# Skipping empty slots in the indirect DMAs, and writing expert rows plainly into a two-half DRAM scratch

## The chip, the cores and the metric

One core of a Trainium2 chip runs the kernel. The metric is the device time of one execution in microseconds (us). The five engines are TensorE (PE, with its weight loads PEld), VectorE (DVE), ScalarE (ACT), GpSimd (POOL) and SyncE (SP). SP computes nothing here: it issues most DMAs. All DMAs of the core run on the same 16 DMA engines; those that SP issues are queue q1 in the profile, those that ACT issues q10, those that POOL issues q0.

## The reference, cut to what matters

One layer for 512 tokens of width 1024: a Mamba-2 mixer, a layer norm, and a mixture of 16 experts in 4 groups. Every token picks one group and 2 experts in it, so there are 1024 assignments. The second half of the computation is what the change touches:

```python
x = layer_norm(DEEPNORM_ALPHA * x + (1.0 + g1) * y, ln1_g[i], ln1_b[i])
hin = (x * (1.0 + sc2) + sh2).reshape(bsz * seq, d)
eid, wts = route(hin, router_w, router_b)          # 2 experts of one group for each token
y = moe_ffn(hin, eid, wts, w_up[i], w_down[i])      # sum over a token's two experts of w * FFN_e(hin)
x = layer_norm(DEEPNORM_ALPHA * x + (1.0 + g2) * y, ln2_g[i], ln2_b[i])
...
def expert_block(args):                             # 128 rows of one expert
    xb, e = args
    gate, up = jnp.split(xb @ w_up[e], 2, axis=-1)  # w_up[e] is 1024 x 2048
    return (jax.nn.silu(gate) * up) @ w_down[e]     # w_down[e] is 1024 x 1024
```

All is float32. Output: (1, 512, 1024) float32.

## The kernel before, in words

**Mixer, then router.** The mixer runs group by group (4 groups of 8 heads) and adds its output into `oacc` in SBUF. Then the first layer norm leaves its rows, without gain and bias, in `xt`, the modulated rows go to the DRAM tensor `h2d` (SP, L389), and the router computes `mask` (which experts a token uses), `wts` and the position of each token among its expert's rows.

**Blocks.** Experts are worked through in blocks of 128 slots, block b being expert b mod 16, `nblk` blocks in all (16 in the profiled run, one for each expert). `tab` holds four columns for each token and expert: token number, the weight in two parts, and the slot in the block. POOL's `select(n)` (L519) compares the slot column to `iota` and makes a 0/1 matrix `sel`; PE's `slot_rows(n)` (L1518) multiplies it by `tabc`, which gives for every slot the token and the weight; DVE's `slots(n)` (L1182) turns that into `idx[:, n]` and `wslot[:, n]`. An empty slot gives a zero, and `dumpc` and the offset in column 0 turn it into a row of its own at or above row 512 (`DUMP`). Both DRAM tensors have 128 such rows more than the 512 tokens need. Slots are filled from partition 0 upward.

**One block.** POOL's `gather(n)` (L508) fetches 128 rows of 4 KB from `h2d` into `xg` by an indirect DMA. PE turns them (`turn_rows`), multiplies by the up weights in 8 units of 1 MB, turns the hidden rows, and multiplies by the down weights in 4 units of 1 MB. Each product is made of three matmuls on a high and a low part: ACT copies a weight unit to its high part (`high`, L749), DVE subtracts it for the low part (`low`, L1118). Weights arrive in a ring of 4 slots of 1 MB (`ring`); SP loads the unit four places later when `low` has released a slot (L379 and L382). The split weights `wr` have 4 slots as well. The order on PE is: up of block b, with `turn_hidden(b-1)` after its unit 1 and `slot_rows(b+2)` after its unit 4, then `turn_rows(b+1)`, then down of block b-1. ACT's `evacuate(b-1)` (L781) scales the result into `yblk` at the end of its turn of block b. POOL's `scatter(b-1)` (L544) adds these 128 rows to the DRAM tensor `ysum` by an indirect DMA with `compute_op=ALU.add`; the next scatter waits for it to land. POOL's order in one turn is `gather(b+1)`, `select(b+2)`, `widen(b)`, `scatter(b-1)`. `widen` puts gain and bias of the first norm on one sixteenth of the columns, from `xt` into `x1`.

**Start values.** `ysum` has to be zero before the first scatter. ACT issues four DMAs of 512 KB for that, and one for the pad rows of `h2d`, at the first mixer group (L724, L726); POOL issues one more (L461). DVE and POOL wait for them (`ld_zero`, `ld_sc`).

**The end.** After the last scatter has landed, SP loads `ysum` in four tiles to `ytok` (L415). DVE multiplies tiles 0 and 2 by the gate row `modr[:, 3]` and POOL tiles 1 and 3 (`gated`, L1264 and L565), DVE forms ALPHA * x1 + ytok (`sums`, L1268), and the second norm follows tile by tile on DVE, ACT and POOL (`scale`, `normalise`, `gain`, `finish`).

## Time and profile before

| | |
|---|---|
| median of 3 runs | 1214.65 us (1210.5 to 1215.7) |
| the profiled execution | 1218.35 us, span 1216.4 us |
| PE busy | 1022.0 us (84%), granted clock 0.935 |
| DVE, ACT, POOL busy | 934.6, 645.8, 461.6 us |
| DMA packets | 289.04 MB; HBM read 272.94 MB, written 15.73 MB |
| q1 (SP's) | 268.77 MB, 60.0% of 16 engines |
| q0 (POOL's) | 17.30 MB, 5.4% of 16 engines |
| q10 (ACT's) | 2.62 MB, 0.5% of 16 engines |
| indirect DMAs | 16 gathers (10.4 us to landing), 16 scatters (11.4 us) |

The span is the time from the first to the last instruction. A share of DMA is the time that packets took, over 16 engines and the span. The mixer fills the span up to about 520 us, the router up to about 568 us, the experts from there to about 1175 us, and the second norm the rest.

### The profile page before, as it was taken

What the parts mean: (1) busy time and instruction counts of PE and PEld (TensorE: products, weight loads), DVE (VectorE), ACT (ScalarE), POOL (GpSimd) and SP (SyncE); (2) the same over time, 40 slices, a digit from 0 to 9 for tenths busy, and PEclk for the clock granted to TensorE, in tenths of its full rate; (3) what the DMA queues carried; (4) which work ended last, traced back from release to release, by engine and by line L of the source; (5) the groups of instructions that cost most, each with busy time, mean ns of one, the idle gap of its engine ahead of it and who ended that gap; (6) DMA issues with size and microseconds to landing.
All of it is one profiled execution on the core that took longest, in us unless ns stands there. A gap on an engine that the chain in (4) does not pass through costs nothing.

```text
span 1216.4 us, 15701 instructions
## 1 busy us (share of the span) xinstructions
PE 1022.0 (84%) x5222; PEld 844.1 (69%) x5222; DVE 934.6 (77%) x985; ACT 645.8 (53%) x599; POOL 461.6 (38%) x313
## 2 busy tenths in 40 slices
PE   0468999989998995853899999999999999999960
PEld 0447778867976974753677887777887778777740
DVE  4586994796599388785598888878888888888848
ACT  0144454345245334141577777667777767767641
POOL 0052554554364355511244422444223444224115
PEclk9988999998999998865899999999999999999985
DMA  4624532532351346043589999999999999999962
GB/s 142 245 87 150 162 88 87 153 106 69 121 169 55 97 145 207 1 175 121 225 336 367 365 373 374 374 353 359 360 381 372 386 361 364 360 365 375 357 206 110
DMA packets 105337, 289.04 MB, mean 238 GB/s; under 512 B 10193, under 2 KB 59481, under 8 KB 87901
## 3 DMA queue, kind: packets, MB, share of 16 engines
q1 hardware_dynamic: 99838, 268.77, 60.0%
q0 software_dynamic: 4752, 17.30, 5.4%
q10 hardware_dynamic: 720, 2.62, 0.5%
q8 instruction: 15, 0.25, 0.1%
q14 instruction: 12, 0.10, 0.0%
HBM read 272.94 MB, written 15.73 MB: 237 GB/s over the span
## 4 chain that ended last, share of the span: by engine, by line
DVE 22%; DMA 21%; PE 12%; issue 7%; ACT 6%; POOL 1%; DVEq 0%; ACTq 0%; SPq 0%; POOLq 0%
DMA moe<-in_moe_w_up 12%; DVE moe_r L1118 9%; DMA moe<-in_moe_w_down 8%; ACT moe_r L749 5%; PE ps L1548 2%; PE ps L1550 2%; PE ps L1552 2%; DVE moe L1210 1%; PE ps L1481 1%; DVE ssd L902 1%; PE ps L1506 1%; PE ps L1483 1%; PE ps L1482 1%; DVE moe_r L1204 1%; DVE ssd L885 1%
## 5 line engine op out<-in xcount | busy, mean ns | idle before, releaser
L1118 DVE TENSOR_TENSOR moe_r<-moe,moe_r 128x2048 fp32r<-128x2048 f32 x192 | 439.1, 2304 | 91.4 <-ACT moe_r L749 89.2
L749 ACT ACTIVATE moe_r<-moe 128x2048 fp32r<-128x2048 f32 x192 | 366.6, 1920 | 155.5 <-DMA moe<-in_moe_w_up 113.0
L1548 PE MATMUL ps<-moe_r 128*128 128x512 f32 x768 | 226.0, 403 | 11.9 <-DVE moe_r L1118 11.3
L1550 PE MATMUL ps<-moe_r 128*128 128x512 f32 x768 | 218.8, 394 | 0.0
L1552 PE MATMUL ps<-moe_r 128*128 128x512 f32 x768 | 216.4, 390 | 0.0
L448 POOL TENSOR_TENSOR ssd_r<-ssd,ssd_r 128x1024 fp32r<-128x1024 f32 x56 | 138.1, 2467 | 155.5 <-ACT ssd_r L592 155.3
L1548 PEld LDWEIGHTS ps<-moe_r 128*128 128x128 f32 x768 | 140.1, 190 | 47.9 <-DVE moe_r L1118 21.6
L1550 PEld LDWEIGHTS ps<-moe_r 128*128 128x128 f32 x768 | 145.9, 190 | 31.6
L1552 PEld LDWEIGHTS ps<-moe_r 128*128 128x128 f32 x768 | 145.0, 189 | 30.8
L544 POOL DMA_INDIRECT ysum<-moe,moe_i x16 | 32.3, 2018 | 330.7 <-ACT moe L781 304.9
L1336 PE MATMUL ps<-ssd_r 128*128 128x512 f32 x320 | 132.4, 414 | 18.1 <-DVE ssd L875 16.3
L1337 PE MATMUL ps<-ssd_r 128*128 128x512 f32 x320 | 127.7, 399 | 0.0
L1338 PE MATMUL ps<-ssd_r 128*128 128x512 f32 x320 | 127.5, 398 | 0.0
L592 ACT ACTIVATE ssd_r<-ssd 128x1024 fp32r<-128x1024 f32 x56 | 58.8, 1052 | 64.7 <-PE ps L1483 60.6
L1336 PEld LDWEIGHTS ps<-ssd_r 128*128 128x128 f32 x320 | 62.1, 194 | 35.5 <-POOL ssd_r L448 10.7
L875 DVE SCALAR_TENSOR_TENSOR ssd<-ps,ssd 128x511 f32<-128x511 f32 (+2 forms) x72 | 53.4, 743 | 36.4 <-ACT ssd L620 34.6
L1481 PE MATMUL ps<-ssd_r 128*128 128x256 f32 x256 | 74.3, 290 | 4.9 <-DVE both L1011 4.3
L470 POOL TENSOR_TENSOR ssd<-ssd 128x384 f32<-128x384 f32 x32 | 49.4, 1544 | 67.6 <-ACT ssd L637 67.6
L1483 PE MATMUL ps<-ssd_r 128*128 128x256 f32 x256 | 74.0, 289 | 0.0
L1482 PE MATMUL ps<-ssd_r 128*128 128x256 f32 x256 | 73.9, 289 | 0.0
L1337 PEld LDWEIGHTS ps<-ssd_r 128*128 128x128 f32 x320 | 62.1, 194 | 14.2 <-issue 1.7
L1338 PEld LDWEIGHTS ps<-ssd_r 128*128 128x128 f32 x320 | 61.8, 193 | 13.7
(246 smaller groups left out, 1456.0 us busy)
## 6 DMA issues: line engine op xcount, KB each, us to landing
moe<-in_moe_w_up SPq DMA_DIRECT2D x128, 1024.0 KB, 6.8
moe<-in_moe_w_down SPq DMA_DIRECT2D x64, 1024.0 KB, 7.0
ssd<-in_ssd_w_in SPq DMA_DIRECT2D x40, 512.0 KB, 4.0
ssd<-in_ada_w SPq DMA_DIRECT2D x32, 512.0 KB, 3.8
ssd<-in_ada_w SPq DMA_DIRECT2D x8, 1024.0 KB, 11.8
ssd<-in_ssd_w_out SPq DMA_DIRECT2D x16, 512.0 KB, 3.5
...
```

Source lines behind the costliest of these rows:

```text
L448: pool.tensor_tensor(wsplit[:, slot, 1, :], stage[:, slot, :], wsplit[:, slot, 0, :].bitcast(F32), ALU.subtract).then_inc(s_ul, 1)
L749: act.activation(wr[:, i % RING, 0, :], ring[:, i % RING, :], ACT.Identity).then_inc(s_wh, 1)
L1118: dve.tensor_tensor(wr[:, i % RING, 1, :], ring[:, i % RING, :], wr[:, i % RING, 0, :].bitcast(F32), ALU.subtract).then_inc(s_wl, 1)
L1336: mm(to, wh[:, k, :], hin[:, 0, k, :], start=(k == 0), stop=False)
L1337: mm(to, wh[:, k, :], hin[:, 1, k, :], start=False, stop=False)
L1338: op = mm(to, wl[:, k, :], hin[:, 0, k, :], start=False, stop=(k == DC - 1))
L1481: mm(to, ysplit[:, 0, k, tt], wh[:, k, :], start=(k == 0), stop=False)
L1482: mm(to, ysplit[:, 0, k, tt], wl[:, k, :], start=False, stop=False)
L1483: op = mm(to, ysplit[:, 1, k, tt], wh[:, k, :], start=False, stop=(k == 3))
L1548: mm(to[i], xh, wh[i], start=start, stop=False)
L1550: mm(to[i], xh, wl[i], start=False, stop=False)
L1552: op = mm(to[i], xl, wh[i], start=False, stop=stop)
```

## The change

Four edits that belong together.

1. An empty slot now gets index 1024 (`ROWS`), above the bound of either indirect DMA (`bounds_check`, `oob_is_err=False`), so it is left out. `h2d` loses its pad rows, and `xg` is set to zero once by POOL.
2. `ysum` becomes `ydram` with 1024 rows: a token's first expert writes to row t, its second to row 512 + t, plainly, without `compute_op`. For this a tensor `order` counts a token's chosen experts within the group before this one, and `tab` gets a fifth column (destination), `idx` a second.
3. The zero fills go, with the waits on them. The router bias is loaded by POOL instead of SP.
4. At the end SP loads the first half (rows 0 to 511) into `xt` as soon as all scatters but the last have landed, and POOL multiplies it by the gate row and adds it to `x1`, tile by tile (`part`). ACT has scaled gain and bias of the first norm by ALPHA, so `sums` is a plain addition. The second half goes through `gated` as `ysum` did.

```diff
+ROWS = 2 * T
-        h2d = nc.dram_tensor("h2d", (T + P, D), F32).ap()
-        ysum = nc.dram_tensor("ysum", (T + P, D), F32).ap()
+        h2d = nc.dram_tensor("h2d", (T, D), F32).ap()
+        ydram = nc.dram_tensor("ydram", (ROWS, D), F32).ap()
...
@@ sync
-            sp.dma_start(rb, router_b.rearrange("(a e) -> a e", a=1).broadcast_to([P, E])).then_inc(ld_r, 16)
...
+            sp.wait_ge(s_first, 1)
+            for t in range(TT):
+                sp.dma_start(xt[:, t, :], ydram[t * P:(t + 1) * P, :]).then_inc(ld_first, 16)
             sp.wait_ge(s_wl, moe_unit(nblk, RING - 1))
             sp.wait_ge(ld_sc, 16 * nblk + 16)
             for t in range(TT):
-                sp.dma_start(ytok[:, t, :], ysum[t * P:(t + 1) * P, :]).then_inc(ld_y[t], 16)
+                sp.dma_start(ytok[:, t, :], ydram[T + t * P:T + (t + 1) * P, :]).then_inc(ld_y[t], 16)
...
@@ gpsimd
-            pool.memset(oacc, 0.0).then_inc(s_zero, 1)
+            pool.memset(oacc, 0.0)
             pool.memset(acc, 0.0).then_inc(s_accz, 1)
-            pool.wait_ge(s_zero, 1)
-            pool.dma_start(ysum[T:T + P, :], oacc[:, 1, :]).then_inc(ld_sc, 16)
...
+            pool.dma_start(rb, router_b.rearrange("(a e) -> a e", a=1).broadcast_to([P, E])).then_inc(ld_sc, 16)
             pool.memset(tab[:, :, BLOCKS:, :], 0.0).then_inc(s_tab, 1)
+            pool.memset(xg, 0.0).then_inc(s_xg0, 1)
             pool.wait_ge(s_nrm, 2)
             pool.tensor_tensor(h2f[1], xt[:, 1, :], modr[:, 2, :], ALU.mult).then_inc(s_h2m, 1)
...
                 pool.indirect_dma_start(xg, None, h2d, bass.IndirectOffsetOnAxis(ap=gix, axis=0),
-                                        bounds_check=T + P - 1, oob_is_err=False).then_inc(ld_g, 16)
+                                        bounds_check=T - 1, oob_is_err=False).then_inc(ld_g, 16)
...
-                pool.indirect_dma_start(ysum, bass.IndirectOffsetOnAxis(ap=six, axis=0), rows, None,
-                                        bounds_check=T + P - 1, oob_is_err=True, compute_op=ALU.add).then_inc(ld_sc, 16)
+                pool.indirect_dma_start(ydram, bass.IndirectOffsetOnAxis(ap=six, axis=0), rows, None,
+                                        bounds_check=ROWS - 1, oob_is_err=False).then_inc(ld_sc, 16)
...
             scatter(final - 1, yblk)
+            pool.wait_ge(s_x1p, 2 * final + 2)
+            pool.wait_ge(ld_sc, 16 * final + 16)
+            pool.sem_inc(s_first, 1)
             scatter(final, ylast)
 
+            def part(t):
+
+                pool.tensor_tensor(xt[:, t, :], xt[:, t, :], modr[:, 3, :], ALU.mult).then_inc(s_part, 1)
+                pool.wait_ge(s_part, 2 * t + 1)
+                pool.tensor_tensor(x1[:, t, :], x1[:, t, :], xt[:, t, :], ALU.add).then_inc(s_part, 1)
+
+            pool.wait_ge(ld_first, 16 * TT)
+            for t in range(TT):
+                part(t)
...
@@ scalar
-            act.wait_ge(s_zero, 1)
-            act.dma_start(h2d[T:T + P, :], oacc[:, 0, :]).then_inc(ld_zero, 16)
-            for t in range(TT):
-                act.dma_start(ysum[t * P:(t + 1) * P, :], oacc[:, 1, :]).then_inc(ld_zero, 16)
...
             act.activation(rstd, rstd, ACT.Silu)
+            act.wait_ge(s_fold, 3)
+            act.activation(lnr, lnr, ACT.Identity, scale=ALPHA).then_inc(s_fold, 1)
...
@@ vector
             link(dve.tensor_copy(whi, wts))
+            mine, nth = quad(mask), quad(order)
+            dve.memset(nth[:, :, 0], 0.0)
+            dve.tensor_copy(nth[:, :, 1], mine[:, :, 0])
+            link(dve.tensor_tensor(nth[:, :, 2], mine[:, :, 0], mine[:, :, 1], ALU.add))
+            link(dve.tensor_tensor(nth[:, :, 3], nth[:, :, 2], mine[:, :, 2], ALU.add))
+            tokb = tokc.unsqueeze(2).broadcast_to([P, TT, E])
+            dve.tensor_copy(tab[:, :, 0:E, 0], tokb)
+            dve.scalar_tensor_tensor(tab[:, :, 0:E, 1], order, float(T), tokb, ALU.mult, ALU.add)
+            dve.tensor_copy(tab[:, :, 0:E, 2], whi.bitcast(F32))
+            dve.tensor_tensor(tab[:, :, 0:E, 3], wts, whi.bitcast(F32), ALU.subtract)
             dve.wait_ge(s_pos, 1)
             link(dve.scalar_tensor_tensor(pm, ps[:, 7, 0:TT * E].rearrange("p (t e) -> p t e", e=E), 1.0, mask, ALU.add, ALU.mult))
-            tokb = tokc.unsqueeze(2).broadcast_to([P, TT, E])
-            pos0 = tab[:, :, 0:E, 3]
-            link(dve.tensor_scalar(pos0, pm, -1.0, None, ALU.add))
-            dve.tensor_copy(tab[:, :, 0:E, 1], whi.bitcast(F32))
-            dve.tensor_tensor(tab[:, :, 0:E, 2], wts, whi.bitcast(F32), ALU.subtract)
-            link(dve.tensor_tensor(tab[:, :, 0:E, 0], tokb, pos0, ALU.subtract))
-            dve.tensor_copy(tabc, tab[:, :, 0, :]).then_inc(s_tabc, 1)
+            link(dve.tensor_scalar(tab[:, :, 0:E, 4], pm, -1.0, None, ALU.add))
+            dve.tensor_copy(tabc[:, :, 0:5], tab[:, :, 0, :]).then_inc(s_tabc, 1)
...
-                dve.tensor_scalar(idx[:, ds(n, 1)], ps[:, 4, 0:1], dumpc, None, ALU.add)
+                dve.tensor_scalar(idx[:, ds(n, 1), :].rearrange("p a c -> p (a c)"), ps[:, 4, 0:2], float(ROWS), None, ALU.add)
...
-                link(dve.scalar_tensor_tensor(xt[:, t, :], x1[:, t, :], ALPHA, ytok[:, t, :], ALU.mult, ALU.add))
+                link(dve.tensor_tensor(xt[:, t, :], x1[:, t, :], ytok[:, t, :], ALU.add))
...
-            dve.wait_ge(s_x1p, 2 * final + 2)
+            dve.wait_ge(s_part, 2 * TT)
             dve.wait_ge(ld_ln, 16 * 4)
             gated(0)
```

## Rows read from the trace of the kernel before

**Rows 1.** Busy time by stretch; the first line names the columns.

```profile
core 0: us, PE busy (x) PEld busy (x) DVE busy (x) ACT busy (x) POOL busy (x), PEclk, DMA share, GB/s
...
900.00:940.00 40.00, 39.72 (x183) 32.23 (x182) 34.20 (x22) 28.82 (x21) 13.97 (x11) 1.00 0.96 363
```

**Rows 2.** DMA queues, 640 to 1140 us: packets, MB, share of 16 engines.

```profile
q1 hardware_dynamic: 29926, 169.41, 86.9%
q0 software_dynamic: 3858, 14.10, 10.7%
```

**Rows 3.** Waits, 640 to 1180 us: engine, line, releaser: total us, times, longest.

```profile
ACT moe_r L749 <- DMA moe<-in_moe_w_up: 107.8, 84, 3.2
...
PEld ps L1548 <- DVE moe_r L1118: 16.0, 25, 1.2
PEld ps L1522 <- POOL moe_r L526: 12.5, 10, 3.0
```

**Rows 4.** The chain that ended last: `hidden` of blocks 1 and 14 (start us, us).

```profile
638.07 1.28 DVE moe L1210 x2
...
1119.43 1.28 DVE moe L1210 x2
```

**Rows 5.** Timeline of PE, block 8: start us, us, engine, line.

```profile
833.83 1.07 PE L1548 MATMUL ps<-moe_r 128*128 128x512 f32 x4
...
836.56 1.03 PE L1541 MATMUL ps<-both,moe 128*128 128x128 f32 x8
837.35 1.17 PE L1548 MATMUL ps<-moe_r 128*128 128x512 f32 x4
```

**Rows 6.** Timeline of ACT and POOL, same block: evacuation, scatter, select.

```profile
832.50 1.11 ACT L781 ACTIVATE moe<-ps,moe 128x1024 f32<-128x1024 f32 x1
...
834.53 1.90 POOL L544 DMA_INDIRECT ysum<-moe,moe_i x1 [21.75 <-ACT moe L781]
...
843.89 4.38 POOL L526 TENSOR_SCALAR moe_r<-both,moe_r 128x128 fp32r<-128x128 f32 x4 [0.21 <-POOL moe_r L522]
```

**Rows 7.** Queue q0 in 568 to 577 us (first gather), 1176 to 1182.5 us (last scatter).

```profile
q0 software_dynamic: 144, 0.52, 14.3%
...
q0 software_dynamic: 144, 0.52, 52.6%
```

**Rows 8.** Timeline of the end, in order of time.

```profile
1167.62 1.60 POOL L544 DMA_INDIRECT ysum<-moe,moe_i  x1 [25.81 <-issue]
...
1173.92 0.18 POOL L540 COPY moe_i<-moe_i 128x1 int32 x1 [4.71 <-DMA ysum<-moe,moe_i]
...
1176.38 1.58 POOL L544 DMA_INDIRECT ysum<-moe,moe_i  x1 [2.28 <-ACT moe L781]
1182.52 1.75 SPq L415 DMA_DIRECT2D moe<-ysum  x4
1186.11 1.22 DVE L1266 TENSOR_TENSOR moe<-moe,both 128x1024 f32<-128x1024 f32 x1 [15.62 <-DMA moe<-ysum]
1187.28 5.62 POOL L567 TENSOR_TENSOR moe<-moe,both 128x1024 f32<-128x1024 f32 x2 [9.31 <-DMA moe<-ysum]
1187.37 3.33 DVE L1272 SCALAR_TENSOR_TENSOR moe<-both,moe 128x1024 f32<-128x1024 f32 x1
...
1202.30 2.34 POOL L571 TENSOR_TENSOR moe<-moe 128x1024 f32<-128x1024 f32 x1 [1.37 <-ACT moe L741]
```

**Rows 9.** Timeline of the router's end on DVE, and ACT's next turn.

```profile
563.20 0.20 DVE L1167 CAST moe_r<-moe 128x64 fp32r<-128x64 f32 x1
563.58 0.23 DVE L1169 SCALAR_TENSOR_TENSOR moe<-ps,moe 128x64 f32<-128x64 f32 x1 [0.18 <-PE ps L1516]
...
577.58 0.60 ACT L766 ACTIVATE moe_r<-ps 128x512 fp32r<-128x512 f32 x1 [18.80 <-PE ps L1532]
```

**Rows 10.** Timeline: ACT's zero fills; POOL ahead of the router.

```profile
116.44 3.79 ACTq L726 DMA_DIRECT2D ysum<-both  x4
...
529.37 3.26 POOL L503 TENSOR_TENSOR both<-moe,both 128x1024 f32<-128x1024 f32 x1 [7.02 <-ACT moe L741]
```

More of the change, by code:

```diff
@@ L37 @@
 MU = DC + DC // 2
-CONSTS = 14
+CONSTS = 13
 RING = 4
 AHEAD = 8
-DUMP = T
+ROWS = 2 * T
 BLOCKS = ROUNDS * E
@@ L65, in sem @@
             return ctx.enter_context(nc.semaphore(name))
-        place = space(ctx, "both", 10126 + 1 + TT, F32)
+        place = space(ctx, "both", 10126 + TT, F32)
         ident = place(P)
@@ L93, in build @@
         shift = place(TT)
-        dumpc = place(1)
         tokc = place(TT)
@@ L173, in build @@
         prob, mask, wts, pm = r3(TT), r3(TT), r3(TT), r3(TT)
-        tab = place(TT * (BLOCKS + 1) * 4).rearrange("p (t b c) -> p t b c", t=TT, c=4)
+        tab = place(TT * (BLOCKS + 1) * 5).rearrange("p (t b c) -> p t b c", t=TT, c=5)
         wslot = place(BLOCKS + 1)
@@ L181, in r4 @@
             return both(w * n, m0[0] - w * n)
-        selp, rank, tie = (r4(TT).rearrange("p (t e) -> p t e", e=E) for _ in range(3))
+        selp, rank, tie, order = (r4(TT).rearrange("p (t e) -> p t e", e=E) for _ in range(4))
         gsum, grank = (r4(TT, EG).rearrange("p (t e) -> p t e", e=EG) for _ in range(2))
@@ L192, in build @@
         sel = place(TT * P).rearrange("p (t s) -> p t s", t=TT)
-        tabc = place(TT * 4).rearrange("p (t c) -> p t c", t=TT)
+        tabc = place(TT * 6).rearrange("p (t c) -> p t c", t=TT)
         whi = place(TT * E).rearrange("p (t e) -> p t e", t=TT)
-        place = space(half, "moe_i", BLOCKS + 1 + 2, I32)
-        idx = place(BLOCKS + 1)
+        place = space(half, "moe_i", 2 * (BLOCKS + 1) + 2, I32)
+        idx = place(2 * (BLOCKS + 1)).rearrange("p (b c) -> p b c", c=2)
         gix = place(1)
@@ L236, in build @@
         s_n, s_fold, s_var1, s_sd1, s_shift, s_nrm, s_om, s_gain, s_done = sems("s_n s_fold s_var1 s_sd1 s_shift s_nrm s_om s_gain s_done")
-        s_h2m, s_h2f, s_x1p, s_zero = sems("s_h2m s_h2f s_x1p s_zero")
+        s_h2m, s_h2f, s_x1p, s_xg0, s_first, s_part = sems("s_h2m s_h2f s_x1p s_xg0 s_first s_part")
         s_h2t, s_h2tc, s_lg, s_mx, s_ex, s_mask, s_pos, s_nblk = sems("s_h2t s_h2tc s_lg s_mx s_ex s_mask s_pos s_nblk")
@@ L429, in _ @@
             pool.iota(iota, pattern=[[1, P]], base=0, channel_multiplier=0, allow_small_or_imprecise_dtypes=True).then_inc(s_const, 1)
[L430 to L432 removed]
+            pool.iota(tokc, pattern=[[P, TT]], base=-ROWS, channel_multiplier=1, allow_small_or_imprecise_dtypes=True).then_inc(s_const, 1)
+            pool.wait_ge(s_const, 5)
             pool.memset(onep[:, 1:2], 0.0).then_inc(s_const, 1)
@@ L440, in _ @@
             sel_of(later, ALU.is_ge, -1, [[-1, 4], [1, 4]], 0).then_inc(s_const, 1)
-            pool.wait_ge(s_const, 11)
+            pool.wait_ge(s_const, 10)
             pool.affine_select(out=gmask, in_=gmask, compare_op=ALU.is_ge, fill=0.0, base=HG - 1,
@@ L512, in gather @@
                     pool.wait_ge(s_xgt, 2 * n)
-                pool.tensor_copy(gix, idx[:, ds(n, 1)]).then_inc(s_gix, 1)
+                pool.tensor_copy(gix, idx[:, ds(n, 1), 0]).then_inc(s_gix, 1)
                 pool.wait_ge(s_gix, n + 1)
@@ L525, in select @@
                 for t in range(TT):
-                    op = pool.tensor_scalar(sel[:, t, :], iota, tabc[:, t, 3:4].bitcast(F32), None, ALU.is_equal)
+                    op = pool.tensor_scalar(sel[:, t, :], iota, tabc[:, t, 4:5].bitcast(F32), None, ALU.is_equal)
                 op.then_inc(s_sel, 1)
@@ L539, in scatter @@
                 pool.wait_ge(ld_sc, 16 * n + 16)
-                pool.tensor_copy(six, idx[:, ds(n, 1)]).then_inc(s_six, 1)
+                pool.tensor_copy(six, idx[:, ds(n, 1), 1]).then_inc(s_six, 1)
                 pool.wait_ge(s_ye, n + 2)
@@ L550, in _ @@
             select(2)
+            pool.wait_ge(s_fold, 3 + 1)
             widen(0, 0)
@@ L1123, in _ @@
             dve.wait_ge(s_lg, TT)
-            dve.wait_ge(ld_r, 32)
+            dve.wait_ge(ld_sc, 16)
             b3 = lambda a, n=E: a.unsqueeze(2).broadcast_to([P, TT, n])
@@ L1250, in _ @@
                 these = slice(r * E, (r + 1) * E)
-                dve.tensor_scalar(tab[:, :, these, 3], pm, float(-1 - P * r), None, ALU.add)
-                dve.tensor_copy(tab[:, :, these, 1], tab[:, :, 0:E, 1])
-                dve.tensor_copy(tab[:, :, these, 2], tab[:, :, 0:E, 2])
-                op = dve.tensor_scalar(tab[:, :, these, 0], tab[:, :, 0:E, 0], float(P * r), None, ALU.add)
+                dve.tensor_copy(tab[:, :, these, 0:4], tab[:, :, 0:E, 0:4])
+                op = dve.tensor_scalar(tab[:, :, these, 4], pm, float(-1 - P * r), None, ALU.add)
             op.then_inc(s_tab, 1)
@@ L1502, in logits @@
                 if t == 0:
-                    pe.wait_ge(ld_r, 32)
+                    pe.wait_ge(ld_r, 16)
                 pe.wait_ge(s_h2tc, 2 * t + 2)
@@ L1521, in slot_rows @@
                 for t in range(TT):
-                    op = mm(ps[:, 4, 0:4], sel[:, t, :], tabc[:, t, :], start=(t == 0), stop=(t == TT - 1))
+                    op = mm(ps[:, 4, 0:4], sel[:, t, :], tabc[:, t, 0:4], start=(t == 0), stop=(t == TT - 1))
                 op.then_inc(s_idxp, 1)
```

16 lines of the change are left out of this document (5 added, 11 removed).

## The prediction

> **What bounds the kernel now.** I read the busy time by stretch first. From 640 us on, while the experts run, PE is busy 39.7 of 40 us at a granted clock of 1.00, the DMA engines have a share of 0.96, and DVE has 34.2 us [rows 1]. Two resources are nearly full at once, so the question is which of them ends last. The queues over 640 to 1140 us say how the DMA engines spend their time: q1 (weights) 86.9% and q0 (gathers and scatters) 10.7%, together 97.6% [rows 2]. The waits say that the DMA is the one: ACT's `high` waits 107.8 us in total for up weights, and this reaches PE in two ways, as 16.0 us of waits for DVE's `low` and 12.5 us for POOL's `select` [rows 3]. The chain of waits gives the pace: `hidden` of block 1 starts at 638.07 and of block 14 at 1119.43, 13 periods of 37.03 us [rows 4].
>
> How far could that fall? PE's own work in a period is 12 units. One takes 833.83 to 836.56, 2.73 us, and one turn of eight transposes takes 836.56 to 837.35, 0.79 us [rows 5]. So 12 x 2.73 + 2 x 0.79, plus about 0.4 for the four narrow matmuls of `slot_rows` (an estimate: half of a turn), is 34.7 us. The period has 2.3 us above that, and (16.0 + 12.5) / 14 = 2.0 of them are the two waits. This 2.3 us is all that relief of the DMA can give; below it PE sets the pace.
>
> **Part 1: the gathers and scatters.** In the loop q0 takes 10.7% of 500 us, 53.5 us of all 16 engines, for 27 indirect DMAs (14.10 MB at 0.52 MB), that is 3.96 us for a gather and a scatter. q1 takes 0.869 x 37.03 = 32.2 us a period [rows 2, 4]. By themselves the two differ: the first gather is 14.3% of 9 us = 1.29 us, the last scatter 52.6% of 6.5 us = 3.42 us for the same 0.52 MB [rows 7]. I put that down to `compute_op`, which reads the destination as well. 1024 assignments in 16 blocks are 64 occupied slots of 128, so half of the rows go, and the plain write should cost like the gather (no row has a plain indirect write; its ends are 0.65 us, and 1.7 us if it keeps the old price for a row). A pair then costs 0.65 + 0.65 = 1.3 us, on the average over the engines. DMA need: 32.2 + 1.3 = 33.5 us, at the present fullness of 97.6% 34.3 us. That lies under PE's 34.7, so PE becomes the bound.
>
> I don't take 34.7, because the wait for `select` has a cause of its own. In one turn the evacuation starts at 832.50, the scatter is issued at 834.53, and `select` ends at 843.89 + 4.38 = 848.27 [rows 6]: 15.8 us. PE reaches `slot_rows` 5 x 2.73 + 0.79 = 14.4 us after it has finished the down weights. Even if ACT evacuates at that very moment this turn would wait 1.4 us; a relieved ACT takes away only its lateness. For all turns I leave 0.4 us, and 0.6 us for bursts that still hold up `low`. Period 35.7 us, gain 1.3 us, over the 14 periods from block 1 to block 15 18.2 us. Ends: 0 (nothing frees) and 2.3 x 14 = 32 us. The turns before block 1, with fewer waits of this kind, give 1.0 us. POOL's own time for an indirect DMA (1.9 us, [rows 6]) may change either way with skipped rows; I take none.
>
> **Part 2: the zero fills.** ACT spends 3.79 us on issuing four fills [rows 10]. DVE is the busier engine at that place and has other things to wait for, so I take 0.3 us; ends 0 and 3.8. POOL's part and its waits stand in idle time.
>
> **Part 3: the router.** POOL gets the `rb` load and the memset of `xg`. It is idle for 7.02 us before its next instruction [rows 10], and two such instructions are a fraction of that; uncovered they would be about 2 us. ACT's scaling of `lnr` (2048 columns, as long as a `high`) stands in its idle 18.80 us [rows 9]. On DVE eight small instructions now stand between the cast at 563.20 and the one at 563.58, which waited 0.18 us only, so nothing covers them. Each is 0.13 to 0.26 us like its neighbours (start to start of these two, less the wait, is 0.20, [rows 9]): 1.3 us, of which 0.2 in the wait; behind it three instructions less return 0.5. Sum +0.6 us, ends 0 and 1.6.
>
> **Part 4: the end.** Here the change adds serial work. DVE's `gated(0)`, at 1186.11 now [rows 8], gets a wait for all eight of POOL's `part` instructions (`s_part`, 8), and queued behind it on DVE is the whole second norm; behind them on POOL stand `gated(1)` and `gated(3)`, for which `sums(1)` and `sums(3)` wait. When can POOL start? The scatter of block 14 is issued at 1167.62 and has landed at 1173.92 [rows 8]. With a cost on the DMA engines of 0.65 to 1.3 us instead of 3.42 it lands about 2.4 us earlier, 1171.5. SP then issues four loads. In the row for `ysum` tile 0 is there 3.59 us after the issue (1182.52 to 1186.11) and tile 1 another 1.17 us later [rows 8], so all four take 3.6 + 3 x 1.17 = 7.1 us: 1178.6. The last scatter, issued at 1176.38 for 1.6 us, is out of POOL's way by then. Eight POOL instructions on 128x1024 at 2.34 us with DVE idle, and four waits between multiplication and addition of 0.2 us each (estimate), are 19.5 us: 1198.1. DVE starts 12.0 us later than now. What the last scatter gains by being plain is worth nothing, for the second half lands long before that. After it, both engines start at once instead of DVE 1.17 us ahead, and 3.33 us for one DVE instruction beside POOL's pair [rows 8] show that they hold each other up: +0.5. Sum +12.5 us, ends +9 (loads overlap better, and the first half is ready at 1176) and +16 (2.81 us an instruction, half of 5.62).
>
> **The sum.** -18.2 - 1.0 - 0.3 + 0.6 + 12.5 = -6.4 us. Against the profiled execution, 1218.35 us (span 1216.4 and 1.95 around it), that is 1212.0. That execution is 3.7 us above the median of the runs, 1214.65, from which the same difference gives 1208.2. I forecast 1208 us.
>
> **Rival A: only half of the DMA engines is relieved.** Slots are filled from partition 0 upward, so the rows that go are those of the upper 64 partitions. If the engines share a transfer by partition, eight of them keep 8 rows each and the other eight have none. A weight unit needs all 16, so the loaded half sets the pace: 32.2 + 1.3 for the gather, unchanged, + 1.3 for a plain scatter = 34.8 us, at 97.6% 35.6, with 0.5 for the wait for `select` 36.1. Gain 0.9 x 14 = 13 us, and the time is 1214.65 - 13 - 1.3 + 13.1 = 1213.5. For it: the order of the slots. Against it: it needs 16 engines in step, and the queues are four units deep. Chance 0.22. The Trainium skill, "DMA: Bandwidth & Descriptors", section "The descriptor swizzle", states this split for a plain 128-partition transfer (partitions 0 to 63 on engines 0 to 7); no row here shows it for an indirect one, and by it alone rival A would hold.
>
> **Rival B: PE at its floor.** Both waits vanish, 2.3 x 14 = 32 us at most, some 28 with a cold stretch left. Time 1214.65 - 28 - 1.3 + 13.1 = 1198.5. For it: need of 34.3 against 34.7. Against it: the 15.8 us of rows 6. Chance 0.17.
>
> **Rival C: slower, by the end.** The place is DVE's wait for `part`, the price 12.5 us (up to 16), and it decides once the loop gives less than 12 us. The loop gives about 3 if skipped rows still occupy the engines as packets of their own, or if POOL's `select` comes later because its indirect DMAs take longer: 1214.65 - 3 - 1.3 + 13.6 = 1224. For it: the end is an addition of counted instructions, the loop only a relief. Against: q0 has 3.96 us in each period and must lose the bytes. Chance 0.14.
>
> **The change does not do what it says:** empty slots are few, or skipped rows are moved anyway. With 64 of 128 used I give it 0.03; it then counts as rival C, at +11 without a gain from skipping and the plain write's gain against it, about 1217.
>
> **How the numbers follow.** Forecast 0.44 (1203 to 1213), A 0.22, B 0.17, C 0.14, the last 0.03. The range takes in B nearly whole and most of C: 1199 to 1222. What can be told from no change is about 0.5%, 6 us, so faster is below 1208.6 and slower above 1220.7. Faster: half of the forecast's cases (0.22), 0.04 of A, B whole: 0.43. Slower: C's 0.13 and 0.02 from the upper edges: 0.15. Same: 0.42.
>
> **What would show it.** Period of `hidden` near 35.7 (A: 36.1, B: under 35.0, C: over 36.7); q0 bytes halved, its share of the loop from 10.7% to 3 to 4%; ACT's wait for up weights under half of 107.8; POOL's eight `part` instructions at 18 to 20 us with DVE idle, and DVE's `gated(0)` 24 us after the last matmul instead of 12. It is wrong if the loop keeps the DMA's pace, if `part` runs beside something that hides it, or if PE's clock in the loop leaves 1.00.

## The result, and the profile after

The kernel after takes 1225.36 us (median of 4 runs, 1222.15 to 1232.29) against 1212.89 us (4 runs, 1210.5 to 1215.7) for the kernel before on the same chip: ratio 1.0078, 95% interval 1.0044 to 1.0113. The change costs 0.8%, and the forecast of 1208 us and its range (to 1222) both miss. The time is that of rival C. Ratios here and below leave out executions in a slower state of the chip, two of the ten of run 2 and one of the kernel before beside runs 9 to 11. The profiled execution took 1228.21 us, span 1226.5, 10.1 more than the span of before.

From the page of the kernel after, engines (busy us, share of the span, instructions), the queues, and the line that scatters:

```profile
PE 1022.3 (83%) x5222; PEld 853.4 (70%) x5222; DVE 935.6 (76%) x984; ACT 648.9 (53%) x600; POOL 504.0 (41%) x321
...
q0 software_dynamic: 4640, 8.41, 1.9%
...
L543 POOL DMA_INDIRECT ydram<-moe,moe_i x16 | 19.7, 1228 | 308.7 <-ACT moe L790 283.5
```

Busy time and bytes did what the diff says: q0 moved 17.30 MB before and moves 8.41 now. The queues of the kernel after from 640 to 1140 us, which answer to [rows 2]:

```profile
q1 hardware_dynamic: 30150, 170.92, 90.8%
q0 software_dynamic: 3888, 7.03, 3.7%
```

q0 fell from 10.7% to 3.7%, so a gather and a scatter together cost 0.037 x 500 / 13.5 = 1.37 us of the 16 engines where they cost 3.96. But q1 rose to 90.8%, with 0.9% more bytes than before: a megabyte of weights took 500 x 0.869 / 169.41 = 2.56 us of 16 engines before and takes 2.66 now. The packets of q0 hardly fell in number either (3858 before, 3888 now). Busy time by stretch, the first stretch that of [rows 1]:

```profile
core 0: us, PE busy (x) PEld busy (x) DVE busy (x) ACT busy (x) POOL busy (x), PEclk, DMA share, GB/s
900.00:940.00 40.00, 39.99 (x187) 32.94 (x186) 34.51 (x22) 30.14 (x22) 17.87 (x11) 1.00 0.96 365
960.00:1000.00 40.00, 35.48 (x154) 28.98 (x153) 31.75 (x21) 26.70 (x19) 17.89 (x11) 0.91 0.97 364
1000.00:1040.00 40.00, 37.15 (x161) 30.54 (x160) 30.78 (x20) 26.11 (x19) 15.50 (x11) 0.91 0.87 325
```

Waits of the kernel after, 640 to 1190 us, beside [rows 3]:

```profile
ACT moe_r L758 <- DMA moe<-in_moe_w_up: 64.6, 72, 2.4
ACT moe_r L758 <- DMA moe<-in_moe_w_down: 35.9, 38, 2.3
...
PEld ps L1534 <- POOL moe_r L525: 17.0, 11, 4.9
...
PEld ps L1560 <- DVE moe_r L1127: 1.1, 3, 0.4
```

PE's waits for DVE's `low` are nearly gone (16.0 to 1.1 us). Its waits for POOL's `select` have grown in this trace (12.5 to 17.0, the longest from 3.0 to 4.9); in a second trace of the same kernel (run 5) they are 10.8, the longest 2.8. DVE's `hidden` in the kernel after, the starts of blocks 0, 1, 11, 12, 14 and 15, beside [rows 4]:

```profile
602.58 1.29 DVE L1224 TENSOR_TENSOR moe<-moe,ps 128x512 f32<-128x512 f32 x2 [7.51 <-ACT moe L785]
640.38 1.28 DVE L1224 TENSOR_TENSOR moe<-moe,ps 128x512 f32<-128x512 f32 x2
...
1004.77 1.28 DVE L1224 TENSOR_TENSOR moe<-moe,ps 128x512 f32<-128x512 f32 x2
1045.74 1.28 DVE L1224 TENSOR_TENSOR moe<-moe,ps 128x512 f32<-128x512 f32 x2
...
1117.92 1.28 DVE L1224 TENSOR_TENSOR moe<-moe,ps 128x512 f32<-128x512 f32 x2
1154.27 1.28 DVE L1224 TENSOR_TENSOR moe<-moe,ps 128x512 f32<-128x512 f32 x2
```

And block 15 in the kernel before:

```profile
1155.90 1.28 DVE L1210 TENSOR_TENSOR moe<-moe,ps 128x512 f32<-128x512 f32 x2
```

From block 1 to block 15 the kernel after takes 1154.27 - 640.38 = 513.9 us. Before it was 517.8 (638.07 to 1155.90), so 14 periods gained 3.9 us in this trace, not 18.2 (run 5 has 14.1, but loses 6.7 from block 0 to 1). Most periods are 34.9 to 36.6 us, one is 37.7, and two in a row are 40.1 and 41.0 (964.7 to 1045.7). The period from block 0 to 1, ahead of the 14, went from 34.1 to 37.8.

The end of the kernel after, a timeline of PE, POOL, SP and DVE, beside [rows 8]:

```profile
1165.03 1.41 POOL L543 DMA_INDIRECT ydram<-moe,moe_i  x1 [25.18 <-issue]
...
1168.72 1.75 SPq L412 DMA_DIRECT2D moe<-ydram  x4
1168.90 0.24 POOL L539 COPY moe_i<-moe_i 128x1 int32 x1 [2.46 <-DMA ydram<-moe,moe_i]
...
1171.98 0.61 PE L1564 MATMUL ps<-moe_r 128*128 128x512 f32 x2
...
1176.52 2.33 POOL L570 TENSOR_TENSOR moe<-moe,both 128x1024 f32<-128x1024 f32 x1 [0.80 <-DMA moe<-ydram]
1177.97 1.74 SPq L416 DMA_DIRECT2D moe<-ydram  x4
1178.94 1.99 POOL L572 TENSOR_TENSOR both<-both,moe 128x1024 f32<-128x1024 f32 x1
...
1192.06 2.00 POOL L572 TENSOR_TENSOR both<-both,moe 128x1024 f32<-128x1024 f32 x1
1194.01 5.62 POOL L580 TENSOR_TENSOR moe<-moe,both 128x1024 f32<-128x1024 f32 x2
1194.09 3.35 DVE L1278 TENSOR_TENSOR moe<-moe,both 128x1024 f32<-128x1024 f32 x1 [24.99 <-POOL both L572]
```

The last matmul ends at 1172.6, and `gated(0)` (L1278) starts 21.5 us later. Before, the last matmul ended at 1174.2 and `gated(0)` came 11.9 us after it:

```profile
1173.63 0.61 PE L1552 MATMUL ps<-moe_r 128*128 128x512 f32 x2
```

DVE stands for 24.99 us and waits for POOL's eight instructions. From the last matmul to the end of the span it is 53.9 us, and was 42.2: +11.7.

The 10.1 us of the span are then: up to `hidden` of block 0 -1.4 (603.95 to 602.58), block 0 to 1 +3.7, the 14 periods -3.9, from there to the last matmul 0, the end +11.7.

### The profile page after: what moved, and what is told of

It is laid out like the page before. It is cut to its first block, busy times and chain, and to the rows that moved or that the text cites. A ratio compares the mean times of both kernels' runs of the same rounds, so it can differ in the third digit from the quotient of the medians.

```text
span 1226.5 us, 15703 instructions
## 1 busy us (share of the span) xinstructions
PE 1022.3 (83%) x5222; PEld 853.4 (70%) x5222; DVE 935.6 (76%) x984; ACT 648.9 (53%) x600; POOL 504.0 (41%) x321
## 3 DMA queue, kind: packets, MB, share of 16 engines
q0 software_dynamic: 4640, 8.41, 1.9%
HBM read 275.04 MB, written 12.58 MB: 235 GB/s over the span
## 4 chain that ended last, share of the span: by engine, by line
PE 34%; DVE 13%; POOL 8%; DMA 6%; issue 6%; ACT 3%; POOLq 0%; DVEq 0%; SPq 0%; ACTq 0%
PE ps L1560 9%; PE ps L1562 9%; PE ps L1564 9%; POOL moe_r L525 3%; DMA moe<-in_moe_w_up 2%; DVE moe_r L1127 2%; DMA moe<-in_moe_w_down 2%; POOL moe L515 1%; ACT moe_r L758 1%; POOL moe_i L512 1%; PE ps L1493 1%; PE ps L1518 1%; DVE ssd L913 1%; PE ps L1495 1%; PE ps L1494 1%
## 5 line engine op out<-in xcount | busy, mean ns | idle before, releaser
L1562 PEld LDWEIGHTS ps<-moe_r 128*128 128x128 f32 x768 | 147.0, 191 | 31.5
L1564 PEld LDWEIGHTS ps<-moe_r 128*128 128x128 f32 x768 | 146.1, 190 | 31.0
L1560 PEld LDWEIGHTS ps<-moe_r 128*128 128x128 f32 x768 | 143.3, 192 | 34.8 <-DVE moe_r L1127 6.7
L543 POOL DMA_INDIRECT ydram<-moe,moe_i x16 | 19.7, 1228 | 308.7 <-ACT moe L790 283.5
L1348 PE MATMUL ps<-ssd_r 128*128 128x512 f32 x320 | 133.2, 416 | 14.4 <-DVE ssd L886 12.6
L1348 PEld LDWEIGHTS ps<-ssd_r 128*128 128x128 f32 x320 | 62.5, 195 | 31.9 <-POOL ssd_r L448 10.7
L525 POOL TENSOR_SCALAR moe_r<-both,moe_r 128x128 fp32r<-128x128 f32 x64 | 80.6, 1271 | 3.4 <-POOL moe_r L521 3.4
L1349 PEld LDWEIGHTS ps<-ssd_r 128*128 128x128 f32 x320 | 62.6, 196 | 14.5 <-issue 1.7
```

The lines of the kernel that those rows point to most:

```text
L525: op = pool.tensor_scalar(sel[:, t, :], iota, tabc[:, t, 4:5].bitcast(F32), None, ALU.is_equal)
L1348: mm(to, wh[:, k, :], hin[:, 0, k, :], start=(k == 0), stop=False)
L1349: mm(to, wh[:, k, :], hin[:, 1, k, :], start=False, stop=False)
L1560: mm(to[i], xh, wh[i], start=start, stop=False)
L1562: mm(to[i], xh, wl[i], start=False, stop=False)
L1564: op = mm(to[i], xl, wh[i], start=False, stop=stop)
```

## The experiments

Two causes were in question for the loop. One is that skipped rows relieve only the DMA engines of the upper slots, as rival A has it. The other is that POOL's `select` comes late. They ask for different cures, and the end has a third. I tried each edit by itself and then together. The theories in the expectations are S (`select` is late), H (half of the DMA engines is relieved) and P (`part` costs the end). Where a table below says "14 periods", it is the time from `hidden` of block 1 to that of block 15 in the profiled execution, as above; ratios are to the kernel before on the same chip, while the traces of different runs can be from different chips. The kernel before has 517.8 there. Two traces of one kernel can differ: by 10.2 us for the kernel after (513.9 and 503.7), by 4.5 for run 4 and its repetition, and by 0.1 for runs 1 and 6, whose loops are the same.

**1. `select` early.** In the kernel after, POOL waits for a block's evacuation and then does scatter, gather and `select` in a row. Here the compares for block b + 3 stand ahead of the scatter, in the time in which POOL waits for the evacuation.

```diff
+            select(3)
             with pool.Fori(1, final) as b:
...
                 gather(b + 1)
-                select(b + 2)
                 widen(pool.snap(b % E), b)
+                select(b + 3)
                 scatter(b - 1, yblk)
```

> The changed kernel with one move: POOL builds the 0/1 matrix of block b+3 while it waits for the evacuation of block b-1, instead of block b+2 after the scatter and the gather. Theory S (the loop gave almost nothing back because select comes late for PE, up to 8.4 us for its four compares, and each long wait of PE is followed by matmuls at half clock): no PE wait for POOL is left, the period of hidden falls from 36.7 us on average to 35.3, and the time from 1225 to about 1203. Theory H (the loop is still paced by the DMA, because only half of the DMA engines was relieved): the wait for POOL goes, but waits for weights take its place, period 36.2, time about 1217.

1217.36 us, ratio 0.9987 (0.9955 to 1.0019). No wait of PE for POOL is left in the loop. The kernel after again (run 5) has 1.0071 (1.0034 to 1.0107): the intervals just part, which would make a late `select` worth about 0.8%, some 10 us; run 6 puts this in doubt. In the traces 14 periods took 507.1 us, 36.2 each, which is the forecast of theory H, as is the time; and block 0 to 1 took 33.4 where the kernel after has 37.8. ACT still waits for weights:

```profile
ACT moe_r L759 <- DMA moe<-in_moe_w_up: 79.1, 83, 2.9
...
ACT moe_r L759 <- DMA moe<-in_moe_w_down: 44.5, 41, 2.7
```

That is 123.6 us for both kinds, against 107.8 + 27.1 in the kernel before. With `select` out of the way, the waits for weights grow, and the DMA sets the pace again.

**2. Occupied slots spread over the partitions.** Slot r now sits in partition 4 (r mod 32) + r div 32, so half-full blocks use all groups of four partitions.

```diff
-            pool.iota(iota, pattern=[[1, P]], ...)
+            pool.iota(iota, pattern=[[1, P // 4], [P // 4, 4]], ...)
```

> The changed kernel with slots numbered so that the occupied ones are spread over all partitions (slot value of column 4b+a is b+32a) instead of filling the lower 64. Same rows, same bytes. Theory H: the DMA engines of the lower partitions carried all rows; now each carries half as much, the last scatter lands faster and keeps nearly all engines busy while it runs, ACT waits less for weights, time 6 to 10 us lower (about 1217). Theory S: the DMA is not what holds the loop, select is as late as before, time 1225 within 4 us.

1224.67 us as the median of the eight executions that count (1226.88 of all ten), ratio 1.0026 (0.9993 to 1.006). By itself this can't be told from the kernel after (1.0071). `select` is late here too, so the relief, if any, can run into that wait. 14 periods took 502.4 us. What the edit does to the DMA engines its last scatter shows, which the part on why the prediction was wrong reads.

**3. `part` on DVE.** The eight instructions of the end move from POOL to DVE, which stood idle, and each tile starts when its own load is there.

```diff
-            pool.wait_ge(ld_first, 16 * TT)
-            for t in range(TT):
-                part(t)
...
-            dve.wait_ge(s_part, 2 * TT)
+            dve.wait_ge(s_x1p, 2 * final + 2)
+            for t in range(TT):
+                dve.wait_ge(ld_first[t], 16)
+                link(dve.tensor_tensor(xt[:, t, :], xt[:, t, :], modr[:, 3, :], ALU.mult))
+                link(dve.tensor_tensor(x1[:, t, :], x1[:, t, :], xt[:, t, :], ALU.add))
```

> The changed kernel with the eight instructions on the first half of the scratch done by DVE, tile by tile as the tiles land, instead of by POOL with DVE waiting for all of them. Theory P (the end costs 12 us because these eight stand in POOL's queue at 2.3 us each while DVE idles): DVE does them in about 10 us from 1172 on, gated(0) starts 9 to 10 us after the last matmul instead of 21.5, time 12 to 14 us lower, about 1212. Rival: the end is late for another reason, the loads of the second half, then gated(0) starts not before 15 us after the last matmul and the time falls by 5 us at most.

1209.82 us, ratio 0.9892 (0.986 to 0.9924), 1.8% below the kernel after. The end in its trace:

```profile
1166.85 0.61 PE L1559 MATMUL ps<-moe_r 128*128 128x512 f32 x2
1167.13 1.23 DVE L1292 TENSOR_TENSOR moe<-moe,both 128x1024 f32<-128x1024 f32 x1 [2.76 <-DMA moe<-ydram]
...
1177.21 1.23 DVE L1269 TENSOR_TENSOR moe<-moe,both 128x1024 f32<-128x1024 f32 x1
1177.40 3.23 POOL L571 TENSOR_TENSOR moe<-moe,both 128x1024 f32<-128x1024 f32 x1 [6.82 <-DMA moe<-ydram]
```

The eight instructions take 10.1 us instead of 17.5 and `gated(0)` starts 9.8 us after the last matmul (ends 1167.5), even sooner than before the change. That is 11.7 us earlier than in the kernel after: 7.4 because DVE is faster at these eight, and 4.3 because the first instruction no longer waits for all four loads, for the edit changes both. From the last matmul to the end it is 40.0 us, where the kernel after has 53.9, so the end returns all that it lost and 2 us more. The ratio fell by more than that: 1.8% are 22 us. In the traces the other 5 to 6 us lie between block 0 and block 15 (546.1 us here, 551.7 in the kernel after), which the edit doesn't touch; why is open.

**4. All three.** Edits 1, 2 and 3 in one kernel.

```diff
+            select(3)
...
-            pool.iota(iota, pattern=[[1, P]], ...)
+            pool.iota(iota, pattern=[[1, P // 4], [P // 4, 4]], ...)
...
+                dve.wait_ge(ld_first[t], 16)
```

> All three edits together. If S, H and P each hold, the period of hidden comes to PE's own 34.7 to 35.0 us, 14 periods give 24 to 28 us and the end 12 to 14: about 1187. If S holds and H does not, the same as select early plus the end on DVE, about 1190. If neither holds, about 1212.

1193.68 us, ratio 0.9777 (0.9746 to 0.9809). 14 periods took 497.3 us, 35.5 each, and not the 34.7 to 35.0 that the three theories together forecast. The time is 7 us above their 1187.

**5. The kernel after again**, for its spread and beside the next runs; nothing is edited.

> The changed kernel itself once more, as the reference for the runs beside it. Slower than the kernel before by 0.4% to 1.1%, as measured first.

1225.12 us, ratio 1.0071 (1.0034 to 1.0107). Here 14 periods took 503.7 us, 36.0 each, with none above 37.4; the two long ones of the first trace don't come back, but block 0 to 1 took 40.8. The late `select` strikes at one turn or another: of the 40.8 this row of its waits, 603 to 641 us, has 5.5 us.

```profile
PEld ps L1534 <- POOL moe_r L525: 5.5, 1, 5.5
```

**6. Early `select` and `part` on DVE, slots not spread.** Edits 1 and 3.

```diff
+                select(b + 3)
...
+                dve.wait_ge(ld_first[t], 16)
```

> The changed kernel with select early and the end on DVE, slots not spread. With the slots spread as well the ratio to the kernel before was 0.978. If spreading the rows over the DMA engines is worth something once POOL is out of the way (theory H), this one is slower than that: ratio 0.983 to 0.988, periods near 36.2 us. If H is empty: ratio 0.978, the same.

1204.17 us, ratio 0.9902 (0.9872 to 0.9932); 14 periods 507.0 us, 36.2 each. Run 3, the same kernel with the late `select`, has 0.9892 (0.986 to 0.9924): here the early `select` returned nothing that can be measured, where run 1 seemed to return 0.8%. By these two pairs a late `select` costs between nothing and about 10 us; which, no run settles.

**7. The same without skipping.** Run 6, but an empty slot again reads and writes a row of its own (rows 1024 + partition, filled with zeros in `h2d`), plainly.

```diff
-                                        bounds_check=ROWS - 1, oob_is_err=False).then_inc(ld_sc, 16)
+                                        bounds_check=ROWS + P - 1, oob_is_err=False).then_inc(ld_sc, 16)
...
-                dve.tensor_scalar(idx[...], ps[:, 4, 0:2], float(ROWS), None, ALU.add)
+                dve.tensor_scalar(idx[...], ps[:, 4, 0:2], dumpc, None, ALU.add)
```

> The kernel with select early and the end on DVE, but empty slots move again: each gets a row of its own above row 1023 in both DRAM tensors, read by the gather and written (plainly) by the scatter; five fills of 512 KB clear the pad rows. Theory B (what counts in the loop is bytes, near 368 GB/s whatever the share of time of each queue): 0.53 MB more in a period is 1.4 us, 20 us over the loop, time 20 us above the same kernel with skipping. Theory C (what counted was the accumulating scatter's time on the engines, 3.4 us against 0.6): without compute_op the unskipped rows cost 0.65 us each way on engines that are not full, and the time is at most 8 us above.

1199.72 us, ratio 0.9856 (0.9797 to 0.9915). Theory B, that the bytes set the pace, would have it 20 us slower and is refuted: moving all rows again costs nothing that can be measured. In the traces it is even ahead (the ratios of the two overlap), 497.4 us for 14 periods against 507.0, and they are strikingly even, 35.2 to 35.6 but for the first (36.9) and the last (36.1). The queues, 640 to 1140 us, first of run 6 and then of this kernel:

```profile
q1 hardware_dynamic: 31181, 174.03, 92.5%
q0 software_dynamic: 3888, 7.03, 3.7%
```

```profile
q1 hardware_dynamic: 31910, 177.05, 90.6%
q0 software_dynamic: 3888, 14.16, 6.9%
```

Skipping takes 3.2 points off q0, yet 500 us carry less weight data with it, 174.03 MB, each at 2.66 us, than without it, 177.05 MB at 2.56 us.

**8. Half of each down unit.** Run 6, but the load of a down unit brings only one of its two rows of weights per partition (the other half of the tile keeps old data, so the down product is not the reference's). All instructions stay.

```diff
-                sp.dma_start(ring[:, j % RING, :].rearrange("p (k n) -> p k n", k=2),
-                             dn_v[ds(e, 1), :, 2 * j:2 * j + 2, :]...)
+                sp.dma_start(ring[:, j % RING, 0:D],
+                             dn_v[ds(e, 1), :, 2 * j:2 * j + 1, :]...)
```

> The kernel with select early and the end on DVE, but each down unit loads only the first half of its 1 MB (the result is not the reference's: half of the down weights are what the ring held). 2.1 MB less in a period of 13.1. If PE's own work is the floor, periods come to 34.7 to 35.0 us and do not go lower, and ACT's waits for weights nearly vanish. If the loop were held by ACT, DVE or the order of waits, the period stays at 35.5 or more.

1186.73 us, ratio 0.9754 (0.9695 to 0.9814). `hidden` of two blocks in a row, where eight of the 14 periods are 34.93 or 34.94:

```profile
841.02 1.28 DVE L1216 TENSOR_TENSOR moe<-moe,ps 128x512 f32<-128x512 f32 x2
875.95 1.28 DVE L1216 TENSOR_TENSOR moe<-moe,ps 128x512 f32<-128x512 f32 x2
```

Halving the loads changes nothing but the DMA, and the period settles there. I read it as PE's floor (the prediction had 34.7), and 14 periods are 487.9 us. So in the loops of runs 1, 4, 6 and 7 it is still the weights that cost what lies above this.

**9. The kernel before with early `select`.** Edit 1 in the kernel before.

```diff
-                select(b + 2)
                 widen(pool.snap(b % E), b)
+                select(b + 3)
```

> The kernel before with select early, nothing else. Its PE waited 12.5 us for POOL. If that was additional to the DMA's pace, the period falls by 0.9 us to 36.1 and the time by 1%. If the DMA with the accumulating scatter sets the pace (4.0 us of q0 in a period, against 2.6 in the kernel without skipping and without compute_op, whose periods are 35.4), it stays at 36.6 to 36.9, the time the same, within 3 us.

1215.95 us, ratio 0.9981 (0.9951 to 1.001). PE's waits for POOL (12.5 us in [rows 3]) are gone, but 14 periods took 517.6 us as before. ACT's wait:

```profile
ACT moe_r L750 <- DMA moe<-in_moe_w_up: 108.8, 86, 3.3
```

In the kernel before a wait for `select` was no loss of its own. PE's waits for DVE's `low` grew instead, from 16.0 to 20.6 us; as I read it, while PE stood the ring filled and the DMA caught up.

**10. Skipping alone.** Run 9 with skipped rows, the accumulating scatter kept.

```diff
-DUMP = T
+DUMP = 2 * T
...
+            pool.memset(xg, 0.0).then_inc(s_zero, 1)
...
-                                        bounds_check=T + P - 1, oob_is_err=True, compute_op=ALU.add).then_inc(ld_sc, 16)
+                                        bounds_check=T + P - 1, oob_is_err=False, compute_op=ALU.add).then_inc(ld_sc, 16)
```

> The kernel before with select early and with empty slots skipped in gather and scatter, the scatter still accumulating into zeroed rows. Theory H (skipping unloads only the half of the DMA engines that do not set the pace): periods as uneven as in the changed kernel (34 to 39 us), no gain over the kernel with select early alone: ratio 0.995 to 1.005. If skipping itself is worth its bytes: ratio 0.98, since 2 us of q0 go from each period.

1211.69 us, ratio 0.9964 (0.992 to 1.0008), 14 periods 512.3 us. q0's share went from 10.8% (run 9) to 5.6%, 1.9 us a pair on the average over the engines, 27 us over 14 periods; 5.3 arrived in the traces, and the ratios of the two runs overlap.

**11. All three again**, on the chip of runs 9 and 10; the edit is that of run 4.

> The changed kernel with select early, the end on DVE and the slots spread, once more on another chip: ratio to the kernel before 0.975 to 0.982 if its first result holds.

1199.96 us, ratio 0.9843 (0.9792 to 0.9894), 14 periods 501.8 us. So all three edits together are 1.6% to 2.2% faster than the kernel before, and 2.3% to 3.0% faster than the kernel after by the ratios of either (0.9777 / 1.0078 to 0.9843 / 1.0071). Run 7 (0.9856), which doesn't skip at all, can't be told from this one, so no run shows that skipping is worth anything on top of the plain scatter.

The loop in one table, worked out from the traces (us; the pair is q0's share of 500 us over 13.5 pairs, over 14 in run 8; the weights are q1's share of 500 us over its MB):

| kernel | `hidden` 0 at | block 0 to 1 | 14 periods | pair on q0 | weights, per MB | ratio |
| --- | --- | --- | --- | --- | --- | --- |
| before | 604.0 | 34.1 | 517.8 | 3.96 | 2.56 | 1 |
| 9 before, early | 597.7 | 32.5 | 517.6 | 4.00 | 2.56 | 0.9981 |
| 10 the same, skipping | 602.6 | 33.9 | 512.3 | 2.07 | 2.64 | 0.9964 |
| after | 602.6 | 37.8 | 513.9 | 1.37 | 2.66 | 1.0078 |
| 5 after again | 603.6 | 40.8 | 503.7 | 1.37 | 2.66 | 1.0071 |
| 1 early | 600.6 | 33.4 | 507.1 | 1.37 | 2.67 | 0.9987 |
| 2 spread | 599.6 | 37.1 | 502.4 | 1.37 | 2.62 | 1.0026 |
| 3 `part` on DVE | 602.8 | 34.3 | 511.8 | 1.37 | 2.66 | 0.9892 |
| 6 early, `part` on DVE | 598.7 | 33.8 | 507.0 | 1.37 | 2.66 | 0.9902 |
| 7 the same, no skipping | 602.8 | 33.6 | 497.4 | 2.56 | 2.56 | 0.9856 |
| 4 all three | 599.6 | 35.4 | 497.3 | 1.37 | 2.63 | 0.9777 |
| 11 all three again | 602.9 | 33.9 | 501.8 | 1.37 | 2.64 | 0.9843 |
| 8 half of down | 599.2 | 32.9 | 487.9 | 1.36 | 2.72 | 0.9754 |

## Why the prediction was wrong

**Right: the end.** Forecast +12.5, measured +11.7. The eight instructions took 17.5 us (forecast 19.5), as the additions took 2.00 us each and not 2.34; and POOL began 3.9 us after the last matmul (forecast 4.4). `gated(0)` came 21.5 us after the last matmul (forecast 24). Run 3 shows the mechanism: on DVE, begun tile by tile, the same work costs nothing net.

**Right: what q0 would show.** Share 3 to 4% forecast, 3.7% measured; a pair 1.3 us forecast, 1.37 measured. PE's floor 34.7 forecast, 34.93 measured (run 8). Fills and router were small, as forecast: `hidden` of block 0 starts 1.4 us earlier, but that says little, since run 9, whose kernel is that of before up to there, starts it at 597.7 and not 604.0.

**Wrong: the loop, -18.2 forecast, -3.9 measured in the first trace and -14.1 in the second.** With the turn from block 0 to 1 it is -19.2 forecast, -0.3 and -7.4 measured. The step that failed reads: a pair costs 1.3 us "on the average over the engines", so the DMA needs 34.3 us, "that lies under PE's 34.7, so PE becomes the bound". The sum took a relief of the average over the engines for a relief of the period, and it left the weights at 32.2 us. In the kernels that skip neither holds. The weights took 2.66 us per MB instead of 2.56, 33.4 us for the 12.58 MB of a period; with 1.37 for the pair the need is 34.8, which at the fullness measured in run 6 (96.2%) is that run's period, 36.2. Rival A gives a reason, that the half of the engines that keeps the rows sets the pace. Three steps between runs, each from one trace a kernel, bear on it:

- Dropping `compute_op` without skipping (run 9 to run 7) lowers the pair by 4.00 - 2.56 = 1.44 us and the period by (517.6 - 497.4) / 14 = 1.45 us. Relief that all engines share arrived in full. (Run 7 also has the changed end and router, which lie outside these periods.)
- Skipping alone (run 9 to run 10, on the same chip) lowers the pair by 1.9 us and the period by 0.38.
- Skipping on top of the plain scatter (run 7 to run 6) lowers the pair by 1.2 us, and the period rises by 0.7. By rival A it would stay; the rise is not explained.

The last scatter of the kernel after shows the packets. Its 144 packets, 1175.9 to 1178.2 us, with the counts of packets by size:

```profile
DMA packets 146, 0.23 MB, mean 102 GB/s; under 512 B 89, under 2 KB 89, under 8 KB 146
...
q0 software_dynamic: 144, 0.23, 26.0%
```

```profile
1176.00:1176.50 0.50, 0.00 (x0) 0.00 (x0) 0.00 (x0) 0.00 (x0) 0.00 (x0) 0.50 0.37 123
1176.50:1177.00 0.50, 0.00 (x0) 0.00 (x0) 0.00 (x0) 0.00 (x0) 0.48 (x1) 0.50 0.47 188
1177.00:1177.50 0.50, 0.00 (x0) 0.00 (x0) 0.00 (x0) 0.00 (x0) 0.50 (x1) 0.50 0.36 147
```

The share never passes 0.47: about half of the engines are at work at any time, at most. Here is the last scatter of before, and then that of run 2, which moves the same 56 rows with the slots spread:

```profile
1178.00:1180.00 2.00, 0.00 (x0) 0.00 (x0) 0.00 (x0) 0.00 (x0) 0.00 (x0) 0.50 0.81 86
1180.00:1182.00 2.00, 0.00 (x0) 0.00 (x0) 0.00 (x0) 0.00 (x0) 0.00 (x0) 0.50 0.90 176
...
1162.50:1163.00 0.50, 0.00 (x0) 0.00 (x0) 0.00 (x0) 0.00 (x0) 0.19 (x1) 0.50 0.88 336
```

With the same rows in other partitions the share reaches 0.88. So it is the partitions of the rows that decide how many engines an indirect DMA uses, as rival A supposed. The Trainium skill, "DMA: Bandwidth & Descriptors", section "The descriptor swizzle", gives partitions 0 to 63 to engines 0 to 7 in a plain transfer; the shares agree with it for an indirect one too, though no view names the single engines. Spreading the slots fits as well (run 6 to run 4: 507.0 to 497.3 us, ratio 0.9902 to 0.9777), but the interval of its second run (0.9843, 501.8 us) overlaps with that of run 6, so this cure is likely and not shown.

Two things keep rival A from being the whole cause. Run 4 has the even relief that the sum assumed, a pair of 1.37 us on all engines, and its period is 35.5 us (35.8 in run 11), not 34.9. That is the period of run 7, which skips nothing and has 1.2 us more on q0. So even relief, too, stopped short here, and the weights, at 2.63 us per MB, took part of it. And the engines' shares in the loop itself were seen by no view. That the relief of q0 did not arrive is shown; that it failed by the uneven load alone is not.

Rival A forecast a period of 36.1 us. Runs 1 and 6, where nothing waits for `select`, have 36.2, and the second trace of the kernel after 503.7 / 14 = 36.0. I gave it 0.22 and placed it at 1213.5 us. Its period was right, partly by luck, as it too left the weights at 32.2 us; what its time lacked is at least in part the next point.

**Wrong in the first trace: `select`, 0.4 us for a turn.** I counted the chain of evacuation, scatter, gather and compares at 15.8 us from [rows 6] against PE's 14.4 us, with one row for the compares, 4.38 us. The kernel after, timeline of POOL, DVE and PE around one turn:

```profile
982.97 8.40 POOL L525 TENSOR_SCALAR moe_r<-both,moe_r 128x128 fp32r<-128x128 f32 x4 [0.21 <-POOL moe_r L521]
982.97 2.31 DVE L1127 TENSOR_TENSOR moe_r<-moe,moe_r 128x2048 fp32r<-128x2048 f32 x1 [1.35 <-ACT moe_r L758]
...
985.21 1.28 DVE L1230 TENSOR_TENSOR moe_r<-ps,moe_r 128x512 fp32r<-128x512 f32 x2
...
986.40 4.57 DVE L1127 TENSOR_TENSOR moe_r<-moe,moe_r 128x2048 fp32r<-128x2048 f32 x2
...
991.42 1.01 PE L1534 MATMUL ps<-moe_r 128*128 128x4 f32 x4 [4.52 <-POOL moe_r L525]
...
992.29 2.05 PE L1560 MATMUL ps<-moe_r 128*128 128x512 f32 x4
```

Four compares that took 4.38 us in [rows 6] take 8.40 here. DVE works without a gap from 982.97 to 990.97, and the last compare ends at 991.37, right behind it. The Trainium skill, "SBUF — State Buffer", section "SBUF: two separate sides", says that a DVE instruction with two inputs from SBUF and a POOL instruction that reads SBUF exclude each other for their whole length. The trace agrees: the compares that run beside DVE's L1230, which has one input from PSUM, take 0.59 us each, and the other two end 0.4 us after a `low` or a pair of them does. PE then stands for 4.52 us, and the four matmuls behind it take 2.05 us where they took 1.07 [rows 5]: after this idle time the granted clock is at its lower level (1.2 GHz, 0.50 from 991.5 to 997 us) where it was at the upper (2.4 GHz, 1.00 from 980 to 988), as the 0.91 of the two stretches 960 to 1040 also shows. This turn has the period of 40.1 us; the next, with a wait of 2.9 us for the same line at 1032, has 41.0. Block 0 to 1, which grew by 3.7 us where 1.0 less was forecast, has such a wait too, of 4.0 us (the forecast's turns before block 1). What this costs the kernel is not settled: taking the wait away returned about 10 us in run 1, and nothing from run 3 to run 6.

Why there are more collisions I can only argue: when the weights come sooner, DVE's `low` stands denser, and POOL finds fewer gaps. The 52 compares between 640 and 1140 us took 53.9 us before, 67.6 after, and 81.3 in run 7, whose loop is the evenest and which hides them; but in the second trace of after (run 5) they took only 56.9.

**Rival C's time, not quite its causes.** Its condition, a loop that gives less than 12 us, was met: the 14 periods and the turn before them gave 0.3 and 7.4 us in the two traces. Of the two causes that I had put there, skipped rows do stay packets, but those cost little (1.37 us a pair); and `select` comes late in some turns, but not because the indirect DMAs take longer (POOL issues a scatter in 1228 ns on average at L543, 2018 before): the compares do. That its time came out is in part luck.

**Open.** Why weight packets take 3.5% longer per megabyte in the kernels that skip is not settled. An uneven load of the engines would let some packets of a unit wait while others are done, but nothing here shows this; run 4, with spread slots, has 500 x 0.930 / 177.02 = 2.63 us, between the 2.66 of run 6 and the 2.56 of run 7, and run 8, where the engines have the least to do, has the most, 2.72. The two traces of the kernel after differ by 10 us in the 14 periods; the turns in which `select` was late account for it (40.1 + 41.0 - 2 x 36.0 = 9), but not why it was late in just these.
